# Two sets of TensorE transposes that were written as matmuls by the identity, in a two-layer decoder step with routed experts

## The reference

```python
act = jax.nn.silu(h1) * h3 * combine[:, :, None].astype(t.dtype)
y = jnp.einsum('tef,efd->td', act, w2)
...
h = h + gate2 * _hier_moe(u, router_group_w[l], ...)
```

## Time and profile before

| | |
|---|---|
| median of 3 runs | 1031.77 us |
| span of the profiled execution | 1035.5 us |
| PE busy | 975.8 us (94%), 5426 matmul records |
| PE weight loads (PEld) busy | 551.6 us (53%) |
| VectorE (DVE) busy | 324.5 us (31%) |
| ScalarE (ACT) busy | 175.1 us (17%) |
| mean granted TensorE clock | 0.959 |
| DMA | 304 GB/s over the span |
| L1496 (`turn_rows`), matmul records | 96 |
| L1485 (`turn_back`), matmul records | 24 |

### The profile page before, as it was taken

How to read it: one execution, slowest core, us unless ns; L and a number is a source line. 1 busy time by engine, 2 the same in 40 slices (tenths; PEclk the granted TensorE clock), 3 DMA queues, 4 the chain that set the end, 5 groups by cost and what they waited for, 6 DMA issues and landing times.

```text
span 1035.5 us, 13316 instructions
## 1 busy us (share of the span) xinstructions
PE 975.8 (94%) x5426; PEld 551.6 (53%) x5426; DVE 324.5 (31%) x833; ACT 175.1 (17%) x388; POOL 40.0 (4%) x68
## 2 busy tenths in 40 slices
PE   7999999999799989999998989999989999998986
PEld 3666655574375665444442546777665444433534
DVE  3141233306442443111110037738543111101024
ACT  2200000003231222111100121054222111101121
POOL 0000000000230000000000020000000000000020
PEclk9999999988879989999999999999989999999987
DMA  9944778727992756999999976315856999999971
GB/s 379 377 163 161 292 279 325 304 102 267 392 356 103 287 201 279 416 421 422 421 423 421 422 292 285 118 45 178 352 207 268 409 422 420 422 422 421 422 268 51
DMA packets 47623, 316.22 MB, mean 305 GB/s; under 512 B 5602, under 2 KB 6002, under 8 KB 12354
## 3 DMA queue, kind: packets, MB, share of 16 engines
q1 hardware_dynamic: 39456, 288.90, 69.2%
q0 software_dynamic: 6096, 22.30, 5.9%
q10 hardware_dynamic: 2002, 4.08, 1.1%
HBM read 303.84 MB, written 11.42 MB: 304 GB/s over the span
## 4 chain that ended last, share of the span: by engine, by line
PE 71%; SPq 11%; DMA 10%; DVE 5%; issue 2%; ACT 1%; POOL 0%; DVEq 0%; POOLq 0%
PE banks L803 25%; PE banks L1404 12%; SPq L417 11%; PE banks L1457 6%; DMA scr<-in_ew 6%; PE banks L1363 5%; PE banks L880 4%; DMA ring<-in_w 3%; PE banks L920 2%; PE banks L867 1%; DMA scr<-yd,row_i 1%; PE banks L1496 1%; PE banks L989 1%; PE banks L1533 1%; PE banks L812 1%
## 5 line engine op out<-in xcount | busy, mean ns | idle before, releaser
L803 PE MATMUL banks<-uT,ring 128*128 128x320 f32 x448 | 124.7, 438 | 2.6 <-DVE uT L1669 2.6
L803 PEld LDWEIGHTS banks<-uT,ring 128*128 128x128 f32 x448 | 85.5, 192 | 42.3 <-issue 7.6
L1404 PE MATMUL banks<-ring,scr 128*64 128x512 f32 x448 | 100.1, 594 | 6.5 <-DMA ring<-in_ew 5.0
L1404 PE MATMUL banks<-scr 128*64 128x512 f32 x416 | 94.2, 602 | 5.0 <-DMA scr<-in_ew 5.0
L1363 PEld LDWEIGHTS banks<-scr 128*128 128x128 f32 (+1 forms) x768 | 75.3, 190 | 14.5 <-issue 12.3
L1363 PE MATMUL banks<-scr 128*128 128x128 f32 (+1 forms) x768 | 81.4, 280 | 0.0
L1404 PEld LDWEIGHTS banks<-ring,scr 128*64 128x64 f32 x448 | 31.9, 137 | 72.5 <-issue 61.7
L615 ACT ACTIVATE scr<-banks,mods 128x128 f32<-128x128 f32 x128 | 36.5, 368 | 182.7 <-PE banks L1363 182.7
L1404 PEld LDWEIGHTS banks<-scr 128*64 128x64 f32 x416 | 31.0, 139 | 65.4 <-issue 58.6
L803 PE MATMUL banks<-ring,uT 128*128 128x512 f32 x128 | 57.0, 598 | 0.0
L803 PE MATMUL banks<-scr,ring 128*128 128x320 f32 x192 | 52.9, 433 | 1.8 <-DVE scr L2433 1.8
(11 more groups left out here) (392 smaller groups left out, 1054.2 us busy)
## 6 DMA issues: line engine op xcount, KB each, us to landing
ring<-in_ew SPq DMA_DIRECT2D x96, 1024.0 KB, 19.6
scr<-in_ew SPq DMA_DIRECT2D x96, 1024.0 KB, 21.4
ring<-in_w SPq DMA_DIRECT2D x80, 1024.0 KB, 8.1
scr<-in_v POOLq DMA_DIRECT2D x16, 256.0 KB, 8.1
yd<-uT POOLq DMA_DIRECT2D x8, 512.0 KB, 8.4
scr<-in_kT POOLq DMA_DIRECT2D x13, 256.0 KB, 7.8
out_hgrn<-scr SPq DMA_DIRECT2D x1, 2304.0 KB, 18.1
scr<-in_s POOLq DMA_DIRECT2D x1, 2048.0 KB, 9.7
```

Of the source, the lines that this page charges most:

```text
L803: last = mm(out, a, b, start=(first and i == 0), stop=(final and i == len(pairs) - 1))
L1404: ins = mm(ps[bank][SLOTS * x:SLOTS * x + SLOTS, :], xe[:, kk, SLOTS * x:SLOTS * x + SLOTS], wab[SLOT[n]][:, x, kk % 4, :], start=(kk == 0 ...
```

## The change

`turn_back` transposes instead of multiplying by the identity, and takes only the r partitions that hold tokens. `turn_rows` keeps its matmul with start=False, so that it still adds to the open sums, and marks it as a transpose. Operands, order, waits and signals are otherwise the same.

```diff
@@ turn_back
                     for t, r in enumerate(TROWS):
-                        ins = mm(ps[7][:, P * t:P * t + r], spread[:, t, :, :].rearrange("p e n -> p (e n)"),
-                                 ident[:, 0:r], start=True, stop=True)
+                        x = spread[0:r, t, :, :].rearrange("p e n -> p (e n)")
+                        ins = pe.transpose(ps[7][:, P * t:P * t + r], x, ident[0:r, 0:r])
                         give(ins, f"back_ps{l}" if t == TT - 1 else None)
@@ turn_rows
-                        give(mm(o, yrows0[t][0:r, P * m:P * m + P], ident[0:r, 0:r], start=False, stop=last), f"out_ps{l}" if last else None)
+                        give(mm(o, yrows0[t][0:r, P * m:P * m + P], ident[0:r, 0:r], start=False, stop=last, is_transpose=True),
+                             f"out_ps{l}" if last else None)
```

## The result

The changed kernel takes 1023.9 us (median of 5 runs, 1020.5 to 1024.3), the one before 1031.77 us beside it. The ratio is 0.9904, with a 95% interval of 0.9884 to 0.9924. Taken off 1031.77 us, the ratio gives 1021.9 us. The forecast was 1025.8 us with a range from 1023.3 to 1029.5. The direction was right and the gain was larger than forecast: 7.9 us by the medians, 9.9 by the ratio, against 6.0. The median lies inside the range, close to its lower end, and the value by the ratio outside it.

A forecast was written before the change was run, and what follows sets the result against it. PE was taken to bound the ends of the experts, full DMA engines the experts themselves. Layer 0's 2.4, layer 1's 3.6 and turn_back's 0 sum to 6.0 us off, giving 1025.8 us, range 1023.3 to 1029.5.

The forecast's parts named there:

- The records: In the turns: a full-size turn falls from two records, 0.224 us, to one of 0.109; eight small ones take 0.5 us.
- Rival 5: An accumulating turn marked as a transpose still makes two records, so only turn_back changes: 1031.5 us; chance 0.03.
- Layer 0 (a): Small turns, end of layer 0's experts: L1530 starts 1.3 us earlier, now waiting for VectorE's copy L1884.
- layer 1 (a): Small turns, end of layer 1's experts: L1530 starts 2.4 us earlier, after copy L1884 ends.
- Steps (c): Wide turns up to the first residual add, each layer: 1.52 us instead of 2.71, 1.2 us saved.
- `turn_back` at 0: Among the experts' pairs: 1.2 us of PE saved but 0 gained, since full DMA engines set the pairs' end.
- step (d): Layer 0's end: VectorE's last-group sum and L1919 (ends 620.52) still have room before L1922 at 621.3.
- Rival 1: Clock at both ends gives nothing back: 5.0 us, 1026.8; or no low clock there: 4.2 us, 1027.6; chance 0.20.
- Rival 2: Clock gives more, as fewer narrow matmuls precede L1533: some 8 us with the turn_backs, 1023.8 us; chance 0.10.
- Layer 0's gain survives the weight stream: Layer 1's experts: PE arriving earlier starts and ends the weight stream earlier, so layer 0's 2.4 us passes through.
- Step (b): Wide products L1530 and L1533, granted clock: 1.2 of 1.3 us kept in layer 0; 2.4 us in layer 1, or 1.4.
- Rivals 3 and 4: Transposes don't hold the clock: 2.5 us gain, 1029.3, chance 0.12; or clock low through both norms: 1036.7, chance 0.05.

The follow-up runs named there:

- back_only: The kernel before with only turn_back transposing, turn_rows still multiplying by the identity; 1034.61 us against 1035.0 us before, ratio 0.9983.
- rows_only: The kernel before with only turn_rows transposing, turn_back left as before; 1024.68 us against 1035.0 us before, ratio 0.9913.
- look_a3: The changed kernel with no edit, traced once more; 1029.16 us, against 1028.37 us for the kernel before of the same pair.
- long_transposes: The changed kernel with 96 more full-size transposes behind turn_rows(1) of layer 0; 1042.73 us in one run.

## Why the prediction was right or wrong, point by point

**The records.** Right, exactly. A turn was forecast to fall from two records to one at 0.109 us, eight small ones to take 0.5 us: measured 1.88 us of loads for 16, and 0.57 us for 8. Rival 5 falls: 48 and 12 records.

**Layer 0 (a), layer 1 (a), the new wait.** Right. L1530 (now L1531) was to start 0.63 us behind the small turns, when VectorE's copy lets it; it is 0.64 in both layers, 0.09 behind the copy's end.

**Steps (c).** Right to 0.06 us: 1.58 us forecast as 1.52. What I didn't foresee is that the norm's first product then waits for ScalarE's square (0.73 us of load idle), since PE is early; it changes nothing on the path, as the sum had the start bound by the square already.

**`turn_back` at 0.** Right as far as it can be told: back_only 0.9983 (0.9953 to 1.0014), and rows_only has the whole gain.

**The room that VectorE has, step (d).** Right. The forecast left VectorE 0.8 us ahead of the first residual add of layer 0. In the traces with the changed turns of rows it waits there between 0 (rows_only) and 1.3 us (look_a3) for PE where the clock stays up, and the end takes 8.38 or 8.39 us in all of them. Rivals 1 and 2 let VectorE's sum bound layer 0 at 1.6 and 3.2 us of gain from where L1919 ended in one trace (620.52). No trace shows such a bound.

**Layer 0's gain survives the weight stream.** Right. From the start of layer 1's experts (first record of L1363) to the small turns it is 230.1, 230.1, 229.5, 229.2 and 229.3 us in the five traces of the kernel before, and 229.3, 229.4, 229.4, 228.8 and 228.7 in the five of after: the stream neither waits out the gain nor adds to it.

**Step (b), the granted clock.** This is the step that failed, and the term that was mis-sized. I took the low stretches of the one trace for those of the kernel, and let the change shift work under them: in layer 0 a fall of the same 3.4 us as before, in layer 1 a rise 2.4 us earlier. At equal clock the two layers save 4.9 us. For the clock the forecast added 1.1 us net, and none in layer 0. The traces of six against six have 2.4 us at the two ends, where the clock is low for a shorter time (layer 1: 3.4 us on the mean instead of 6.8; layer 0: 1.1 instead of 2.8, which is not clear of chance). The pooled runs have about 3.3 us in all. So of the 2.9 us that the forecast of 6.0 lacks against 8.9, some 2.2 are the clock, and 0.7 stay open, less than the standard error. The one trace also was a poor sample: it had 2 x 0.041 x 1035.5 = 85 us at 1.2 GHz, against a mean of 74.6 us over the runs.

Rival 2 named less time at the low clock, with a shorter run of narrow matmuls ahead of the wide ones, and gave it 0.10. Its 1023.8 us is the number closest to the measurement, but in part by luck: it was added up with `turn_back`'s 0.9 us and VectorE's bound, and no run shows either. Why the clock falls less is not shown: no run took the narrow matmuls away alone, and with the small turns changed alone layer 1 still had 6.8 us at 1.2 GHz.

**The range.** Its lower end was rival 2 with a bit more, from single stretches. The spread from one execution to the next, 1028.5 to 1038.6 us for the same kernel before in one session, was wider than the three runs shown (1031.14 to 1034.85), and belonged in it.

**Rivals 3 and 4.** Fallen by long_transposes, and by the clock at 1.00 from 617.1 to 621.3 us in the trace of after. **Rival 1** had 5.0 us, or 4.2 with no low clock at all. Its idea, that the clock gives nothing back, is worth 4.9 us by the stages; the timed 8.9 with a standard error of 0.9 excludes each of these.

## What to carry to other kernels

Count records, not durations, when a float32 matmul by the identity is turned into a transpose: it becomes one record instead of two, also where it accumulates, and it is worth what the path holds of them, 2.46 us for 24 turns here and nothing that could be measured for the six of a layer in a stretch bound by DMA. Size it from stages at equal granted clock. A single trace of a kernel whose clock falls now and then can be several us off in one stage (10.84 to 15.78 us for the same instructions here), so trace the kernel before more than once and put that spread into the range. That the clock falls less behind shorter work on PE is what the runs suggest here, and it may not carry over.

## What the runs showed of the hardware that I had not expected

- A float32 transpose of 128 x 128 takes 0.109 us and one of 64 x 64 0.06 us, in series, at 2.4 GHz, with accumulation as without. Over 96 of them in a row the clock was at 2.4 GHz (one trace).
- The same 80 records at the end of layer 1's experts took 10.84, 14.10 or 15.78 us in executions of the same instructions, with 0, 6.8 or 10.3 us at 1.2 GHz.
- An execution is about 0.33 us longer for each microsecond that the mean granted clock puts at 1.2 GHz; a stage bound by PE alone loses 0.5 (12.52 us with 3.4 of them low, against 10.84).
